# The chunked delta-rule scan: keys transposed as full tiles, with the second key operand's chunks exchanged

## The chip, the cores and the metric

One core of a Trainium2 chip runs the whole program as one launch. The metric is the device time of one execution in microseconds. Everything is float32.

## The reference, cut to what matters

The program is a model of six layers on 512 tokens (and 256 context tokens) of width 1024. The change touches one layer, an RWKV-7 mixer, whose core is a recurrence over 768 tokens, in two directions, with 16 heads of 64:

```python
def step(S, inp):
    w_t, k_t, v_t, kk_t, a_t = inp[:5]
    s_kk = jnp.einsum('nbhvk,nbhk->nbhv', S, kk_t)
    S = S * w_t[..., None, :] - s_kk[..., :, None] * (kk_t * a_t)[..., None, :] + v_t[..., :, None] * k_t[..., None, :]
    y_t = jnp.einsum('nbhvk,nbhk->nbhv', S, inp[5]) if emit else None
    return S, y_t
```

S is a 64x64 state per head. There are two kinds of keys that write into it: `k_t` (called kd below), with the value beside it, and `kk_t * a_t` (called ka below), with the difference beside it that the state is corrected by.

## The kernel before, in words

The recurrence is computed in chunks of 64 tokens. Twelve scan steps (`SCAN_STEPS`, L2286) alternate between the two directions n = 0 and n = 1; each takes a tile of 128 tokens, which is two chunks c = 0, 1 (`HALF`, L2288: columns or partitions 0 to 63 and 64 to 127). Keys lie in SBUF with features on the partitions: 8 groups p (two heads of 64 features each), and 128 tokens along the free dimension, as `KA`, `KD` (the two kinds of keys) and `AR` (kk and r), [128 x 8 x 128] each.

Per step s the work has three strands, each written as a generator on every engine, and `scan_slots` (L2343) takes their pieces in a fixed order that each engine has for itself (a string of "1", "2", "c"):

- strand 1, `chosen_*`, for step s + 2: four groups of decay sums on TensorE (L2435), exponentials on ScalarE (L2649, L2650), products of the operands with them on VectorE (L2750 kk, L2753 KA, L2759 KD, L2761 r), the matrix L from AR and KA on TensorE (L2448), its copy by ScalarE (L2659), and the inverse of its 16x16 diagonal blocks on VectorE (stream transposes L2769, small products L2780 to L2846, four scaled copies on ScalarE L2664, transposes back L2794, L2797).
- strand 2, `solved_*`, for step s + 1: the 64x64 triangular inverse from those blocks. `blocks` (masked by VectorE, L2879, and one addition on GpSimd, L2973), the series Z2 and Z3 (L2484 and 64x64 products; ScalarE copies L2676), the inverse Q (copy L2703), the Gram products `values` (L2533; masked by VectorE, L2893), and between them the two token groups, `tokens(0)` and `tokens(1)` (L2505).
- strand c, `carried_*`, for step s: the state products chunk by chunk (X, U, P, Y), with ScalarE's copies of X (L2718) and of U (L2726) and VectorE's sums into the state (L2935; scaling between steps L2925) and the output (L2943).

A token group turns the keys of one chunk c into rows of tokens, for the state product P. On TensorE it is 16 products with the identity as moving operand: the 64 columns of KD's chunk give the partitions HALF[c] of a PSUM bank, the 64 columns of KA's chunk the partitions HALF[1 - c]. Two banks (halves of the 8 groups) are filled, and ScalarE copies each with one 128x512 copy to `KB[s % 2][c]` (L2685). The value rows `VU` have the values on the partitions HALF[c] and the differences on HALF[1 - c], hence that layout. Banks of strands 1 and 2 come in turn from a ring of four (`take(pl, x, "0123")`, L250): the Z2 series of the first eight heads takes the two banks that `tokens(0)` doesn't have, that of the other eight heads takes the two of `tokens(0)` and waits (`free`) for ScalarE's copies of them. `product` is one matmul call (L334); `turned` (L338) is a transpose call (L340).

TensorE's order of the pieces is "1 1 c 2 1 1 2 c 2 c 2 2 c 1 c c 2 2 c 2 2 c 2 2 2" (L2420): decay sums, two; a state piece; `blocks(0)`; decay sums, two; `blocks(1)`; a state piece; `tokens(0)`; a state piece (U); Z2 twice; P and Y; L; X of the second chunk, twice a piece; `tokens(1)`; Z3; U; Z3; the Gram product G; P and Y; Q; the last two Gram products. ScalarE's is "1 1 1 1 c 2 c 2 2 1 c 2 2 c 2 1 2" (L2636): its token copies stand just ahead of the copies of U (L2726), those ahead of the copies of Z2.

SyncE issues the loads. `keys_sp` (L2360) waits until the last Gram product of two steps before has read the tiles, then loads ka and kd, a contiguous 4 KB on each of 128 partitions each; `rows_sp` (L2370) behind it loads kk and r in pieces of 512 B; then come a value load (L2401), the decays' load (L2357) and a value load. VectorE waits for kk at L2750 and for KA at L2753, once a step.

Of the kernel before, what the change touches and what calls it, by code (L numbers as in the profile page):

```python
# [10 lines left out]
ALU = mybir.AluOpType  # L11
ACT = mybir.ActivationFunctionType
AX = mybir.AxisListType.X

P = 128
# [245 lines left out]
def bank(pl, key):  # L261
    return pl.banks[pl.bank_of[key]]
# [59 lines left out]
def table(pl, name, lo=0, hi=None):  # L322
    at, n = pl.coff[name]
    return pl.C[:, at + lo:at + (n if hi is None else hi)]
# [7 lines left out]
def product(e, out, pairs, start=True, stop=True, loose=False):  # L332
    for i, (a, b) in enumerate(pairs):
        r = e.matmul(out, a, b, start=start and i == 0, stop=stop and i == len(pairs) - 1, skip_group_check=loose)  # L334
    return r


def turned(pl, e, out, in_):  # L338
    k = in_.shape[0]
    return e.transpose(out, in_, table(pl, "ident")[0:k, 0:k])  # L340
# [288 lines left out]
QI, KI, GL, GQ, GK, QA, KA, UC, RB, VB, VA, TILES = 0, 2, 3, 4, 5, 6, 10, 14, 16, 18, 22, 26  # L629
# [1658 lines left out]
HALF = slice(0, 64), slice(64, 128)  # L2288
# [71 lines left out]
def keys_sp(pl, e, s):  # L2360
    S_, b = pl.S, pl.scan
    n, tile = SCAN_STEPS[s]
    if s >= 2:
        e.wait_ge(*S_.gram.at(s - 2, "last"))
    for name, dst, signal in ((f"ka{n}", b.KA[s % 2], (S_.ska0, S_.ska1)[s % 2]),
                              (f"kd{n}", b.KD[s % 2], (S_.skd0, S_.skd1)[s % 2])):
        e.dma_start(dst, pl.F[name][tile].rearrange("p (m c) -> p m c", m=8)).then_inc(*signal.next(s))


def rows_sp(pl, e, s):  # L2370
# [53 lines left out]
def chosen_pe(pl, e, s, ring="0123"):  # L2424

    S_, b = pl.S, pl.scan
    n, _ = SCAN_STEPS[s]
    for j in range(4):
        at = ("decays", s, j)
        ps = take(pl, at, ring)  # L2430
        if j == 0:
            e.wait_ge(*S_.slw.at(s))
        e.wait_ge(*free(pl, at))
        for i in range(2):
            t = e.matmul(ps[:, 256 * i:256 * i + 256], b.LW[:, P * (2 * j + i):P * (2 * j + i) + P],  # L2435
                         table(pl, f"tri{n}"), start=True, stop=True)
        t.then_inc(*S_.decay_sums.next((s, j)))
        yield
    at = [("L", s, par) for par in range(2)]
    ps = [take(pl, x, ring) for x in at]  # L2440
    e.wait_ge(*S_.dve_operands.at(s, "al"))
    e.wait_ge(*S_.dve_operands.at(s, "be"))
    for par in range(2):
        e.wait_ge(*free(pl, at[par]))
    for p in range(8):
        for c in range(2):
            for par in range(2):
                t = product(e, ps[par][HALF[c], 64 * p:64 * p + 64],  # L2448
                            [(b.AR[s % 3][HALF[par], p, 0, HALF[c]], b.KA[s % 2][HALF[par], p, HALF[c]])])
    t.then_inc(*S_.gram.next((s, "L")))  # L2450
    yield


def solved_pe(pl, e, s):


    S_, b = pl.S, pl.scan
    AR, KA, KD, KB = b.AR[s % 3], b.KA[s % 2], b.KD[s % 2], b.KB[s % 2]
# [43 lines left out]
                                [(b.T16[HALF[c], 8 * g + hh, :], b.Z1[HALF[c], 8 * g + hh, :])])  # L2502
        t.then_inc(*S_.inverse_made.next((s, "Q")))

    def tokens(c):  # L2505
        names = [("tokens", s, c, hf) for hf in range(2)]
        ps = [take(pl, x, "0123") for x in names]
        if c == 0:
            e.wait_ge(*S_.dve_operands.at(s, "ka"))
        for x in names:  # L2510
            e.wait_ge(*free(pl, x))
        for p in range(8):
            o = ps[p // 4][:, P * (p % 4):P * (p % 4) + P]
            product(e, o[HALF[c], :], [(KD[:, p, HALF[c]], table(pl, "ident"))])
            t = product(e, o[HALF[1 - c], :], [(KA[:, p, HALF[c]], table(pl, "ident"))])
        t.then_inc(*S_.operands_turned.next((s, c)))

    def values(c):

        names = [("gram", s, c, par) for par in range(2)]  # L2520
        ps = [take(pl, x, "0123") for x in names]
        e.wait_ge(*S_.dve_operands.at(s, "ka" if c is None else "ro"))
        for x in names:
            e.wait_ge(*free(pl, x))
        for p in range(8):
            for i in range(2):
                for par in range(2):
                    cols = slice(64 * p, 64 * p + 64)
                    if c is None:
                        t = product(e, ps[par][HALF[i], cols], [(KD[HALF[par], p, HALF[i]],  # L2530
                                                                 AR[HALF[par], p, 0, HALF[i]])])
                    else:
                        t = product(e, ps[par][HALF[1 - c if i else c], cols],  # L2533
                                    [((KA if i else KD)[HALF[par], p, HALF[c]], AR[HALF[par], p, 1, HALF[c]])])
        t.then_inc(*S_.gram.next((s, "G") if c is None else (s, "R", c), *([(s, "last")] if c == 1 else [])))

    blocks(0)
# [131 lines left out]
def solved_act(pl, e, s):  # L2669
    S_, b = pl.S, pl.scan  # L2670

    def series(g, stage, dst):
        e.wait_ge(*S_.inverse_made.at(s, g, stage))
        for c in range(2):
            at = (stage, s, g, c)
            e.activation(dst[HALF[c], 8 * g:8 * g + 8, :], by_heads(bank(pl, at)[HALF[c], :]), ACT.Copy).then_inc(  # L2676
                *S_.act_blocks.next((s, g, stage), frees=at) if c else S_.act_blocks.next(frees=at))

    def tokens(c):
        e.wait_ge(*S_.operands_turned.at(s, c))  # L2680
        if s >= 2:
            e.wait_ge(*S_.carried.at(2 * (s - 2) + 1, "P"))
        for hf in range(2):
            at = ("tokens", s, c, hf)
            e.activation(b.KB[s % 2][c][:, 512 * hf:512 * hf + 512], bank(pl, at)[:, :], ACT.Copy).then_inc(  # L2685
                *S_.act_turned.next((s, c), frees=at) if hf else S_.act_turned.next(frees=at))

    tokens(0)
    yield
    for g in range(2):  # L2690
        series(g, "Z2", b.Z2)
        yield
    tokens(1)
    yield
    for g in range(2):
        series(g, "Z3", b.Z1)
        yield
    e.wait_ge(*S_.inverse_made.at(s, "Q"))
    if s >= 2:
        e.wait_ge(*S_.carried.at(2 * (s - 2) + 1, "U"))  # L2700
    for c in range(2):
        at = ("Q", s, c)
        e.activation(b.Q[s % 2][:, 8 * c:8 * c + 8, :], by_heads(bank(pl, at)[:, :]), ACT.Copy).then_inc(  # L2703
            *S_.act_blocks.next((s, "Q"), frees=at) if c else S_.act_blocks.next(frees=at))
    yield
# [36 lines left out]
def chosen_dve(pl, e, s):  # L2742
    S_, b = pl.S, pl.scan
    n, _ = SCAN_STEPS[s]
    AR, KA = b.AR[s % 3], b.KA[s % 2]
# [4 lines left out]
    e.tensor_tensor(AR[:, :, 0, :], AR[:, :, 0, :], b.E[:, :, 0, :], ALU.mult).then_inc(*made.next((s, "al")))  # L2750
    e.wait_ge(*S_.decayed.at(s, 3, "m"))
    e.wait_ge(*(S_.ska0, S_.ska1)[s % 2].at(s))
    e.tensor_tensor(KA, KA, b.EM, ALU.mult).then_inc(*made.next((s, "be")))  # L2753
    e.tensor_copy(b.EL[:, s % 4, :], b.E[:, :, 1, last]).then_inc(*made.next())
    e.reciprocal(b.EF[:, s % 4, :], b.E[:, :, 0, 127 - last]).then_inc(*made.next((s, "ends")))
    yield
# [1264 lines left out]
```

## Time and profile before

| | us |
|---|---|
| median of 3 runs | 4994.42 |
| lowest, highest | 4991.78, 4994.98 |
| the profiled execution | 4992.55 |
| its span, first to last instruction | 4990.7 |
| TensorE busy | 4795.9 |
| VectorE busy | 1474.0 |
| ScalarE busy | 1054.5 |

The span is what the profile's rows add up to; the execution's own time is 1.85 us longer. PE is TensorE's matmuls, PEld its weight loads (they overlap), DVE is VectorE, ACT ScalarE, POOL GpSimd, SPq the queue of SyncE that issues DMAs. A float32 product on TensorE stands as two records. In a timeline row the columns are the start, the time from the first start to the last end, engine, line, operation, tiles and shapes, count, and in brackets the idle time before it and what ended it; W and A are SBUF, C the constants, ps PSUM. The matmuls of all helpers have the helper's line, L334 or L340, so they are told apart by shapes and place.

### The profile page before, as it was taken

How to read it: one execution, taken by the hardware profiler on the slowest of the kernel's cores; microseconds unless marked ns; L12 is line 12 of the kernel's file. 1: busy time of each engine (PE TensorE's matmuls, PEld its weight loads, DVE VectorE, ACT ScalarE, POOL GpSimd, SP SyncE). 2: the span in 40 equal slices, each digit the busy share in tenths (PEclk: the TensorE clock that was granted, in tenths of full speed). 3: DMA queues.
4: the chain of work that ended last, by engine and by line, in shares of the span. 5: the costliest groups of instructions: out<-in, count | busy, mean ns of one | idle time of the engine just before them, and what ended most of it. 6: DMA issues, size and time to landing. Idle time of an engine off the chain costs nothing.

```text
span 4990.7 us, 63120 instructions
## 1 busy us (share of the span) xinstructions
PE 4795.9 (96%) x27502; PEld 2627.9 (53%) x27502; DVE 1474.0 (30%) x2777; ACT 1054.5 (21%) x2046; POOL 322.4 (6%) x302
## 2 busy tenths in 40 slices
PE   8999999999999999999999989998999999999999
PEld 4444444444444444666545568887544555544444
DVE  3621110363111010000044337775301444410100
ACT  1131000113100022111033124443211333311210
POOL 1100000020000000000003200000000011000000
PEclk9989999998999999999999999999999999999999
DMA  3151212115121211111134322222211000111211
GB/s 122 60 203 68 76 65 78 62 57 213 59 76 69 75 51 68 51 43 51 53 128 137 128 94 76 73 78 97 77 50 52 28 15 28 44 51 68 84 67 59
DMA packets 91840, 378.36 MB, mean 76 GB/s; under 512 B 7984, under 2 KB 33712, under 8 KB 62128
## 3 DMA queue, kind: packets, MB, share of 16 engines
q1 hardware_dynamic: 80608, 332.92, 18.9%
q0 software_dynamic: 9808, 37.75, 2.2%
q8 instruction: 219, 3.59, 0.3%
q10 hardware_dynamic: 1152, 3.67, 0.2%
q14 instruction: 53, 0.43, 0.0%
HBM read 334.46 MB, written 39.85 MB: 75 GB/s over the span
## 4 chain that ended last, share of the span: by engine, by line
PE 92%; DVE 4%; ACT 2%; issue 1%; DMA 0%; POOL 0%; POOLq 0%; SPq 0%; DVEq 0%; ACTq 0%
PE ps L522 43%; PE ps L334 23%; PE ps L543 7%; PE ps L3414 2%; PE ps L1782 2%; PE ps L340 1%; PE ps L3336 1%; PE ps L991 1%; PE ps L947 1%; PE ps L3425 1%; PE ps L3339 1%; PE ps L2435 1%; PE ps L2484 1%; PE ps L3335 1%; PE ps L3337 1%
## 5 line engine op out<-in xcount | busy, mean ns | idle before, releaser
L522 PE MATMUL ps<-A,W 128*128 128x512 f32 (+1 forms) x5344 | 2150.1, 562 | 23.9 <-DVE A L494 8.8
L522 PEld LDWEIGHTS ps<-A,W 128*128 128x128 f32 x5344 | 1018.0, 192 | 1105.7 <-issue 1063.4
L334 PE MATMUL ps<-A,W 64*64 64x64 f32 (+3 forms) x3264 | 660.9, 379 | 9.4 <-ACT A L3579 5.8
L334 PEld LDWEIGHTS ps<-A,W 128*128 128x128 f32 (+2 forms) x3264 | 349.0, 162 | 304.3 <-issue 280.7
L334 PEld LDWEIGHTS ps<-A 64*64 64x64 f32 (+2 forms) x8416 | 400.6, 147 | 148.7 <-issue 93.9
L334 PE MATMUL ps<-A 64*64 64x64 f32 (+3 forms) x8416 | 437.8, 237 | 41.1 <-ACT A L2650 14.1
L543 PE MATMUL ps<-W,A 128*128 128x512 f32 (+1 forms) x896 | 367.0, 571 | 1.8 <-ACT A L1568 1.8
L543 PEld LDWEIGHTS ps<-W,A 128*128 128x128 f32 x896 | 173.0, 194 | 191.2 <-issue 183.7
L436 ACT ACTIVATE A<-R 128x512 f32<-128x512 f32 (+1 forms) x96 | 52.6, 574 | 758.5 <-DVE R L1578 330.5
L1698 DVE SCALAR_TENSOR_TENSOR A<-ps,V,A 128x512 f32<-128x512 f32 (+1 forms) x48 | 31.0, 661 | 486.9 <-PE ps L334 486.3
L1578 DVE SCALAR_TENSOR_TENSOR R<-ps,MOD,R 128x512 f32<-128x512 f32 (+1 forms) x48 | 31.7, 662 | 416.5 <-PE ps L522 410.5
L3558 ACT ACTIVATE A<-ps,A 128x256 f32<-128x256 f32 (+1 forms) x128 | 84.9, 668 | 283.3 <-DVE A L3679 283.3
L1714 POOL TENSOR_TENSOR A<-A 128x1536 f32<-128x1536 f32 (+1 forms) x16 | 46.4, 2900 | 1488.9 <-ACT A L1671 1488.9
L1512 DVE TENSOR_TENSOR A<-A,ps 128x512 f32<-128x512 f32 x44 | 30.2, 688 | 334.0 <-PE ps L522 334.0
L1671 ACT ACTIVATE A<-ps 128x256 f32<-128x256 f32 (+1 forms) x96 | 50.3, 527 | 369.8 <-PE ps L522 369.7
L334 PE MATMUL ps<-W,A 64*64 64x64 f32 (+3 forms) x1472 | 117.9, 260 | 1.2 <-issue 0.8
L334 PEld LDWEIGHTS ps<-W,A 64*64 64x64 f32 (+1 forms) x1472 | 101.9, 163 | 21.7 <-issue 16.5
L3677 DVE TENSOR_REDUCE A<-ps 128x1 f32<-128x256 f32 (+1 forms) x128 | 71.4, 558 | 132.6 <-PE ps L3337 132.0
L340 PE MATMUL ps<-C,A 128*128 128x128 f32 x608 | 97.1, 284 | 10.9 <-DVE A L1250 10.3
L1479 ACT ACTIVATE A<-ps 128x512 f32<-128x512 f32 x44 | 26.3, 598 | 369.8 <-PE ps L522 369.8
L340 PEld LDWEIGHTS ps<-C,A 128*128 128x128 f32 x608 | 70.0, 141 | 60.7 <-issue 41.7
L1517 DVE TENSOR_TENSOR R<-R,ps 128x512 f32<-128x512 f32 x16 | 11.0, 688 | 300.0 <-PE ps L334 300.0
(362 smaller groups left out, 4234.8 us busy)
## 6 DMA issues: line engine op xcount, KB each, us to landing
W<-in_ada SPq DMA_DIRECT2D x48, 1024.0 KB, 5.5
W<-in_w_up SPq DMA_DIRECT2D x44, 1024.0 KB, 4.8
W<-in_w_down SPq DMA_DIRECT2D x32, 704.0 KB, 4.0
W<-in_w_in SPq DMA_DIRECT2D x18, 1024.0 KB, 4.8
W<-in_sgu_v SPq DMA_DIRECT2D x16, 1024.0 KB, 4.9
W<-in_sgu_u SPq DMA_DIRECT2D x16, 1024.0 KB, 4.8
W<-in_sgu_z SPq DMA_DIRECT2D x16, 1024.0 KB, 4.8
W<-in_sgu_o SPq DMA_DIRECT2D x16, 1024.0 KB, 4.8
```

The lines of the kernel that those rows point to most:

```text
L334: r = e.matmul(out, a, b, start=start and i == 0, stop=stop and i == len(pairs) - 1, skip_group_check=loose)
L340: return e.transpose(out, in_, table(pl, "ident")[0:k, 0:k])
L436: e.activation(pl.sq[k % 2][:, cols], pl.R[:, k, cols], ACT.Square).then_inc(*S_.act_squares.next((key, k, seg[0])))
L522: t = e.matmul(ps, w[:, k, c:c + mc], x(k, seg), start=k == 0, stop=k == kt - 1)
L543: mm = e.matmul(ps, x(k0 + k, tile), w[:, k, :], start=k0 + k == 0, stop=k0 + k == kt - 1)
L947: e.matmul(ps, b.qa[o:o + 64, pair, P * i:P * i + P], b.ka[o:o + 64, pair, 0:L], start=True, stop=True).then_inc(*S_.att_scores.next((l, n)))
L991: t = e.matmul(ps[32 * k:32 * k + 32, :], b.cs[:, 4 * hf + k, :], w[:, k, :], start=hf == 0, stop=hf == 1)
L1671: e.activation(dst[:, m, o:o + seg[1]], bank(pl, at)[:, 0:seg[1]], func).then_inc(*signal.next((i, g), frees=at) if m == 1 and seg is segs ...
L1782: t = e.matmul(y, w[:, k, :], b.x(k, s), start=k == 0, stop=k == 7)
L3414: t = e.matmul(ps[:, :], uq[j][:, k, 0:P], b.cq[:, k, :], start=k == 0, stop=k == 5)
L3558: e.activation(b.pr[:, z, lo:hi], bank(pl, at)[:, 0:hi - lo], ACT.Exp, bias=m[:, 2:3], scale=b.rq[:, p % 2, 2 * i + j:2 * i + j + 1], accu ...
L3677: e.tensor_reduce(m[:, part:part + 1], bank(pl, at)[:, 0:w], AX, ALU.max).then_inc(*made.next())
```

## The change

A token group no longer stands for a chunk but for half of the key groups (hf): four groups p, each turned by two full 128x128 transposes (`turned`), KD into one bank and KA into another. For KA's rows to come out on the partitions HALF[1 - c], KA is loaded with its two chunks exchanged: two DMAs instead of one, each of pieces of 64 tokens (256 B). What reads KA follows: the product with the exponentials is cut into two halves, and L and the Gram products read the exchanged half. ScalarE copies each bank in two halves of 64 partitions, as the halves go to different `KB[..][c]`: four copies a group instead of two.

```diff
@@ -2362,9 +2362,11 @@
     n, tile = SCAN_STEPS[s]
     if s >= 2:
         e.wait_ge(*S_.gram.at(s - 2, "last"))
-    for name, dst, signal in ((f"ka{n}", b.KA[s % 2], (S_.ska0, S_.ska1)[s % 2]),
-                              (f"kd{n}", b.KD[s % 2], (S_.skd0, S_.skd1)[s % 2])):
-        e.dma_start(dst, pl.F[name][tile].rearrange("p (m c) -> p m c", m=8)).then_inc(*signal.next(s))
+    ka, signal = pl.F[f"ka{n}"][tile].rearrange("p (m c) -> p m c", m=8), (S_.ska0, S_.ska1)[s % 2]
+    for c in range(2):
+        e.dma_start(b.KA[s % 2][:, :, HALF[1 - c]], ka[:, :, HALF[c]]).then_inc(*signal.next(s) if c else signal.next())
+    e.dma_start(b.KD[s % 2], pl.F[f"kd{n}"][tile].rearrange("p (m c) -> p m c", m=8)).then_inc(
+        *(S_.skd0, S_.skd1)[s % 2].next(s))
 
 
 def rows_sp(pl, e, s):
@@ -2446,7 +2448,7 @@
         for c in range(2):
             for par in range(2):
                 t = product(e, ps[par][HALF[c], 64 * p:64 * p + 64],
-                            [(b.AR[s % 3][HALF[par], p, 0, HALF[c]], b.KA[s % 2][HALF[par], p, HALF[c]])])
+                            [(b.AR[s % 3][HALF[par], p, 0, HALF[c]], b.KA[s % 2][HALF[par], p, HALF[1 - c]])])
     t.then_inc(*S_.gram.next((s, "L")))
     yield
 
@@ -2502,18 +2504,18 @@
                                 [(b.T16[HALF[c], 8 * g + hh, :], b.Z1[HALF[c], 8 * g + hh, :])])
         t.then_inc(*S_.inverse_made.next((s, "Q")))
 
-    def tokens(c):
-        names = [("tokens", s, c, hf) for hf in range(2)]
+    def tokens(hf):
+
+        names = [("tokens", s, hf, k) for k in range(2)]
         ps = [take(pl, x, "0123") for x in names]
-        if c == 0:
+        if hf == 0:
             e.wait_ge(*S_.dve_operands.at(s, "ka"))
         for x in names:
             e.wait_ge(*free(pl, x))
-        for p in range(8):
-            o = ps[p // 4][:, P * (p % 4):P * (p % 4) + P]
-            product(e, o[HALF[c], :], [(KD[:, p, HALF[c]], table(pl, "ident"))])
-            t = product(e, o[HALF[1 - c], :], [(KA[:, p, HALF[c]], table(pl, "ident"))])
-        t.then_inc(*S_.operands_turned.next((s, c)))
+        for p in range(4):
+            for k, keys in enumerate((KD, KA)):
+                t = turned(pl, e, ps[k][:, P * p:P * p + P], keys[:, 4 * hf + p, :])
+        t.then_inc(*S_.operands_turned.next((s, hf)))
 
     def values(c):
 
@@ -2530,8 +2532,9 @@
                         t = product(e, ps[par][HALF[i], cols], [(KD[HALF[par], p, HALF[i]],
                                                                  AR[HALF[par], p, 0, HALF[i]])])
                     else:
-                        t = product(e, ps[par][HALF[1 - c if i else c], cols],
-                                    [((KA if i else KD)[HALF[par], p, HALF[c]], AR[HALF[par], p, 1, HALF[c]])])
+                        to = HALF[1 - c if i else c]
+                        t = product(e, ps[par][to, cols],
+                                    [((KA if i else KD)[HALF[par], p, to], AR[HALF[par], p, 1, HALF[c]])])
         t.then_inc(*S_.gram.next((s, "G") if c is None else (s, "R", c), *([(s, "last")] if c == 1 else [])))
 
     blocks(0)
@@ -2676,14 +2679,16 @@
             e.activation(dst[HALF[c], 8 * g:8 * g + 8, :], by_heads(bank(pl, at)[HALF[c], :]), ACT.Copy).then_inc(
                 *S_.act_blocks.next((s, g, stage), frees=at) if c else S_.act_blocks.next(frees=at))
 
-    def tokens(c):
-        e.wait_ge(*S_.operands_turned.at(s, c))
+    def tokens(hf):
+        e.wait_ge(*S_.operands_turned.at(s, hf))
         if s >= 2:
             e.wait_ge(*S_.carried.at(2 * (s - 2) + 1, "P"))
-        for hf in range(2):
-            at = ("tokens", s, c, hf)
-            e.activation(b.KB[s % 2][c][:, 512 * hf:512 * hf + 512], bank(pl, at)[:, :], ACT.Copy).then_inc(
-                *S_.act_turned.next((s, c), frees=at) if hf else S_.act_turned.next(frees=at))
+        for k in range(2):
+            at = ("tokens", s, hf, k)
+            for c in range(2):
+                to = HALF[1 - c if k else c]
+                e.activation(b.KB[s % 2][c][to, 512 * hf:512 * hf + 512], bank(pl, at)[to, :], ACT.Copy).then_inc(
+                    *S_.act_turned.next(*([(s, hf)] if k else []), frees=at) if c else S_.act_turned.next())
 
     tokens(0)
     yield
@@ -2750,7 +2755,9 @@
     e.tensor_tensor(AR[:, :, 0, :], AR[:, :, 0, :], b.E[:, :, 0, :], ALU.mult).then_inc(*made.next((s, "al")))
     e.wait_ge(*S_.decayed.at(s, 3, "m"))
     e.wait_ge(*(S_.ska0, S_.ska1)[s % 2].at(s))
-    e.tensor_tensor(KA, KA, b.EM, ALU.mult).then_inc(*made.next((s, "be")))
+    for c in range(2):
+        x = KA[:, :, HALF[1 - c]]
+        e.tensor_tensor(x, x, b.EM[:, :, HALF[c]], ALU.mult).then_inc(*made.next((s, "be")) if c else made.next())
     e.tensor_copy(b.EL[:, s % 4, :], b.E[:, :, 1, last]).then_inc(*made.next())
     e.reciprocal(b.EF[:, s % 4, :], b.E[:, :, 0, 127 - last]).then_inc(*made.next((s, "ends")))
     yield
```

## Rows read from the trace of the kernel before

**Rows 1.** The page: busy time of each engine; the ending chain by engine.

```profile
PE 4795.9 (96%) x27502; PEld 2627.9 (53%) x27502; DVE 1474.0 (30%) x2777; ACT 1054.5 (21%) x2046; POOL 322.4 (6%) x302
...
PE 92%; DVE 4%; ACT 2%; issue 1%; DMA 0%; POOL 0%; POOLq 0%; SPq 0%; DVEq 0%; ACTq 0%
```

**Rows 2.** One window: PE, PEld, DVE, ACT, POOL busy, clock, DMA share, GB/s.

```profile
3080.00:3120.00 40.00, 37.26 (x965) 33.01 (x966) 32.47 (x55) 17.72 (x36) 2.18 (x2) 1.00 0.24 67
```

**Rows 3.** Chain that ended last, two scan steps: start, duration, what.

```profile
3097.60 0.03 ACT A L2659
...
3124.71 0.14 issue
...
3151.30 1.72 ACT A L2664 x4
```

**Rows 4.** Timeline around the first token group, and one group of copies.

```profile
3087.78 1.97 PE L334 MATMUL ps<-C,W 128*64 128x128 f32 x32
...
3089.68 0.97 PE L334 MATMUL ps<-A 64*64 64x64 f32 x26
3089.79 1.09 ACT L2685 ACTIVATE A<-ps 128x512 f32<-128x512 f32 x2 [3.17 <-PE ps L334]
...
3090.90 1.08 ACT L2726 ACTIVATE A<-ps 64x512 f32<-64x512 f32 x2
...
3092.29 0.60 PE L2484 MATMUL ps<-C 64*64 64x512 f32 x1
...
3092.66 1.21 ACT L2676 ACTIVATE A<-ps 64x512 f32<-64x512 f32 x2 [0.68 <-PE ps L334]
...
L2676 ACT ACTIVATE A<-ps 64x512 f32<-64x512 f32 x96 | 56.8, 592 | 33.2 <-PE ps L334 32.0
```

**Rows 5.** Timeline: second token group, and the ends of two steps.

```profile
3101.35 1.97 PE L334 MATMUL ps<-C,W 128*64 128x128 f32 x32
...
3115.90 1.97 PE L2435 MATMUL ps<-C,A 128*128 128x256 f32 x8 [1.20 <-DVE A L2893]
...
3150.48 0.69 DVE L2846 TENSOR_REDUCE A<-A 128x64 f32<-128x512 f32 x1
...
3157.53 1.97 PE L2435 MATMUL ps<-C,A 128*128 128x256 f32 x8 [0.93 <-DVE A L2893]
```

**Rows 6.** Timeline of the features stage: full transposes between matmuls.

```profile
2797.47 0.82 PE L340 MATMUL ps<-C,A 128*128 128x128 f32 x6
2798.13 2.31 PE L334 MATMUL ps<-A,W 128*128 128x512 f32 x5
```

**Rows 7.** Timeline of VectorE: products of other sizes, and its wait.

```profile
3106.11 1.03 DVE L2834 TENSOR_TENSOR A<-A 128x512 f32<-128x512 f32 x1
...
3134.76 1.41 DVE L2925 TENSOR_TENSOR A<-A 64x512 f32<-64x512 f32 x2
3137.60 1.40 DVE L2935 TENSOR_TENSOR A<-A,ps 64x512 f32<-64x512 f32 x2 [1.44 <-PE ps L334]
```

**Rows 8.** Loads: KB, us to landing; their issue and their first user.

```profile
A<-f_kk SPq DMA_DIRECT2D x4, 512.0 KB, 8.0
...
W<-f_kk SPq DMA_DIRECT2D x1, 512.0 KB, 6.1
W<-f_r SPq DMA_DIRECT2D x1, 512.0 KB, 7.9
...
3116.04 0.56 SPq L2377 DMA_DIRECT2D W<-f_kk  x1
...
3129.86 1.23 DVE L2750 TENSOR_TENSOR W<-W,A 128x1024 f32<-128x1024 f32 x1
```

**Rows 9.** TensorE's first block products in two steps; one window.

```profile
3118.92 2.10 PE L334 MATMUL ps<-A 64*64 64x64 f32 x64
...
3411.79 3.56 PE L334 MATMUL ps<-A 64*64 64x64 f32 x64 [1.76 <-DVE A L2893]
...
3410.00:3420.00 10.00, 5.21 (x104) 5.04 (x105) 6.36 (x10) 0.00 (x0) 1.08 (x1) 0.78 0.01 2
```

## The prediction, made before the changed kernel was built

> **What bounds the kernel now.** I read the page first: TensorE is busy for 96% of the span and holds 92% of the chain that ended last [rows 1]. An average over stages says nothing of one stage, so next come windows over the scan. It runs from about 2870 to 3470 us, in twelve steps of some 42 us; in an ordinary stretch of 40 us TensorE is busy 37, at full granted clock, VectorE 32 and ScalarE 18 [rows 2]. The third view is the chain of waits through two steps, with the timeline of single engines beside it [rows 3 to 5]. In each step it has two parts. From the decay sums (3115.90) to the solve's input matrix L, the chain stays on TensorE, and the first token group (`tokens(0)`) lies in it. From ScalarE's copy of L (3097.60) to the next decay sums it lies on VectorE and ScalarE: the blocks' inverse, four scaled copies (L2664), the transposes, and a masking (L2893) that frees a PSUM bank for the decay sums. The second token group (`tokens(1)`, from 3101.35) lies under that part in the steps of direction 1. In the steps of direction 0 VectorE's inverse is shorter, and the chain comes to L2664 by way of TensorE and ScalarE's series copies, but only just: VectorE had its result at 3150.48 + 0.69 = 3151.17 and ScalarE began L2664 at 3151.30 [rows 3, 5]. So time saved in `tokens(0)` should reach the end, and time saved in `tokens(1)` mostly turns into idle TensorE ahead of the decay sums.
>
> **Turning the keys.** A token group is 16 products of 128x64 keys with the identity; a float32 product stands as two records, so 32 records. They start at 3087.78 and the next group at 3089.68: 1.90 us, 59 ns a record. The second group (3101.35) takes the same 1.97 us to its last end [rows 4, 5]. The new group is 8 calls of `turned` on full 128x128 tiles. Six such calls exist in the features stage: six records, 0.82 us to the last end, and the next matmul starts 0.66 us after the first, so 0.110 us each [rows 6]. There a call is one record, each with other data. Eight take 0.88 us: 1.02 us less a group. The bounds: zero gain if the tile cost what 8 x 2 records of 128x256 pace do (1.97/8 = 0.246 us for 256 columns [rows 5], half of it for 128, so 16 x 0.123 = 1.97 us), and 1.02. I take 1.02, since [rows 6] show this very form.
>
> **Copies on ScalarE.** Two copies 128x512 a group (a pair in 1.09 us) become four of 64x512. Pairs of this size take 1.08 us where both write the same half of the partitions (L2726) and 1.21 where they alternate (L2676) [rows 4]. One alone is 0.59 us, so one follows another every 0.49 to 0.62 us. In the first group the transposes would end at 3087.78 + 7 x 0.11 + 0.27 = 3088.82, ScalarE starts at 3088.86, and four copies end between 3090.92 (3 x 0.49 + 0.59) and 3091.31 (3 x 0.62 + 0.59). Before, they ended at 3090.88. Queued behind them on ScalarE are the U copies (L2726), so these start at most 0.4 us later than 3090.90, and the state products that want them start well after 3092.29. The second Z2 series takes the two banks that the copies free. TensorE reaches it at 3092.29 now, at 3091.27 then; a bank comes free 0.14 us after the copy (the step from ScalarE to TensorE in the chain, [rows 3]), at 3091.06 to 3091.45. The new wait is 0 to 0.18 us; I take 0.09. After `tokens(1)` the same sum gives a wait only in time that is idle anyway. The copy of L (3097.60) follows TensorE. So **tokens(0)** gives 12 x (1.02 - 0.09) = 11.2 us.
>
> **tokens(1)** gives 0.1 us in each of some five steps of direction 0 (3151.30 less 3151.17, [rows 5]), nothing in those of direction 1, and its whole 1.0 in the last solved step, which has no step behind it whose inverse VectorE would work on: 1.5 us.
>
> **VectorE.** The product KA*EM, 1.22 us, is cut in two of 128x512. Above, two products over half the partitions take 1.40 us (L2925), so 0.2 us more; the farthest row, a 128x512 product of another pattern (L2834), takes 1.03, two of them 0.84 us more. Behind it stand the Q and state scalings, and then VectorE waits 1.44 us for TensorE (3137.60, [rows 7]); with that wait shorter by 0.93 there is 0.5 left, so 0.2 costs nothing and 0.84 would cost 0.34 a step, 4 us in all. I take 0.2, as the pieces of 256 bytes lie side by side in the same tiles. The Gram products change only which half of KA they read: same shapes, same count.
>
> **Loads.** One issue more on SP a step, and its 128 packets of 4 KB become 2 x 1024 of 256 B. Behind them on SP's queue stand kd, kk, r and the values. Of those, kk (1024 packets of 512 B, issued at 3116.04) landed after 6.1 us, and r, issued 0.6 us behind it, after 7.9 [rows 8]; so such a load adds 2.4 us to the queue. Two halves at that price, less nothing for the load they replace, are 4.8 us late; at the price of bytes nearly none. kk landed at 3122.1 and is wanted at 3129.86 (L2750), so 7.7 us of cover, and 5.8 by the median landing of 8.0 [rows 8]; ka, issued first, and r, wanted later, have more. Cost 0; a microsecond of lateness beyond the cover would cost a microsecond a step. The values are issued a step ahead, and the decays' load waits for TensorE to 3123.82.
>
> **Clock.** The idle time of TensorE before the decay sums is 1.20 us in one direction, 0.93 in the other [rows 5]; it grows to some 2.2 and 1.8. No ordinary step shows a lower clock now. But in the last solved step TensorE was idle for 1.76 us before 3411.79, the granted clock went to its lower level (1.2 GHz; 0.78 mean over 3410 to 3420) and 64 records took 3.56 us where they take 2.10 otherwise: 1.46 us lost, on the chain [rows 9]. So some steps will now pay: between none and all twelve. The one fall had 1.76 us of idle time before it, and none came after 1.20; I take three steps, at 1.1 us each since part falls on idle time: 3.3 us.
>
> By the Trainium skill (TensorE: Matmul & The Clock Gate, Part 4, PE-mode transpose) transposes on TensorE do not count as activity for the clock gate as matmuls do. No row here shows it: the transposes of [rows 6] stand between dense matmuls. It speaks against this change: by it the sum would go towards rival C, by the rows it stands.
>
> **The sum.** 11.2 + 1.5 - 3.3 = 9.4 us. The profiled execution took 4992.55 us (span 4990.7), so 4983.2; the median of the runs shown is 1.9 above it, so 4985.1. I predict 4985.
>
> **Rivals.** (A) *The clock stays up*: TensorE's longer idle time is spread over two places and the level never falls. Gain 12.7, 4981.7. For it: the 37 of 40 us busy. Against it: the fall behind 1.76 us of idle time. 0.27. (B) *ScalarE becomes the bound*, or VectorE's cut product does: the second Z2 series waits for banks, and the copy of L moves by half or less. At 0.6 us or more lost a step the gain is 0 to 5; 4989 to 4994. Against it: ScalarE has 0.68 us of idle time before the next L2676 pair [rows 4]. 0.14; a transpose dearer than in [rows 6] is in here too. (C) *The clock pays at every step*: with half the records in the token groups the lower level comes in each step, once or twice. At 12 to 20 times 1.46 the 12.7 are turned into a loss of 5 to 16: 5000 to 5010; with eight times, a gain of 1: 4993. 0.09. The page named above is what this rival rests on if transposes count for nothing. (D) *The slower side by the loads*: kk comes after VectorE is ready at L2750. It decides from 5.8 us of added queue time on. At twice the 2.4 us for each half, 9.6 less 1.3 for the replaced packets is 8.3, late by 2.5 a step, 30 a run, against 9.4 gained: 5005. For it: packets of 256 B exist nowhere in these loads. Against it: nothing shows twice the price. 0.05. The Trainium skill (DMA: Bandwidth & Descriptors, the table at its head) says that below 512 B the engines read, modify and write.
>
> **How the numbers follow.** Forecast 0.45 (own range 4981 to 4988), A 0.27, B 0.14, C 0.09, D 0.05. A measurement of this kernel tells some 0.2%, 10 us, from no change. Faster by more: all of A and a good third of the forecast's, 0.43. Slower by more: D and about half of C, 0.09. The rest, 0.48, is within. The range 4979 to 4995 takes in A with 2 us beside it, the forecast, B and the mild end of C.
>
> **What would show it.** 576 TensorE records fewer (24 x 24); `turned` groups of 8 in 0.88 us at L340; ScalarE four copies in 2.1 to 2.5 us; step period down from 42 to about 41.2; idle before the decay sums near 2 us; granted clock under 1 in a few steps; kk landing one to five us later, with VectorE at L2750 still released by ScalarE. Wrong if the period is unchanged, if L2750 waits for a DMA, or if the clock in the scan falls everywhere.

## The result, and the profile after

The changed kernel takes 4986.05 us (median of 20 runs, 4976.62 to 4992.24); the kernel before, in 20 runs beside it, 4992.58. The ratio is 0.9986, interval 0.9979 to 0.9992: 6.5 us faster (4 to 10 by the interval), less than the 10 us that I called telling. The profiled execution took 4983.66 us, its span is 4981.9.

The page of the changed kernel, busy times and chain by engine (answers to [rows 1]):

```profile
PE 4775.0 (96%) x26926; PEld 2606.3 (52%) x26926; DVE 1474.1 (30%) x2789; ACT 1080.2 (22%) x2094; POOL 322.4 (6%) x302
...
PE 90%; DVE 6%; ACT 2%; issue 2%; DMA 0%; POOL 0%; POOLq 0%; DVEq 0%; ACTq 0%; SPq 0%
```

TensorE has 576 records fewer, ScalarE 48 more, as the change says. The chain has moved from TensorE to VectorE by 2% of the span.

The timeline around the first token group, the same step as [rows 4]:

```profile
3082.01 1.04 PE L340 MATMUL ps<-C,W 128*128 128x128 f32 x8
...
3082.99 0.97 PE L334 MATMUL ps<-A 64*64 64x64 f32 x26
3083.09 2.31 ACT L2690 ACTIVATE A<-ps 64x512 f32<-64x512 f32 x4 [2.14 <-PE ps L340]
3083.28 1.29 DVE L2760 TENSOR_TENSOR A<-A 128x512 f32<-128x512 f32 x2
...
3085.42 1.08 ACT L2731 ACTIVATE A<-ps 64x512 f32<-64x512 f32 x2
...
3085.60 0.60 PE L2486 MATMUL ps<-C 64*64 64x512 f32 x1
...
3088.87 1.40 DVE L2942 TENSOR_TENSOR A<-A,ps 64x512 f32<-64x512 f32 x2 [0.36 <-PE ps L334]
```

The next group starts 0.98 us after the first transpose; before, it started 1.90 us after the first product. ScalarE's four copies take 2.31 us. The second Z2 series starts 3.59 us after the token group began, 4.51 before (3092.29 - 3087.78): 0.92 us saved. VectorE's cut product takes 1.29 us instead of 1.22 (L2753 before), and VectorE still waits 0.36 us for TensorE afterwards, where it waited 1.44 us in the same step before.

How far does that carry? A yardstick inside the scan is the time from the first to the last copy of L by ScalarE, twelve pairs of copies; the instructions of that line, with their first and last start, in the kernel before and the changed one:

```profile
L2659 ACT ACTIVATE A<-ps x24: 591/594/603, 2902.3 to 3392.6; 128x512 f32<-128x512 f32 x24
```

```profile
L2662 ACT ACTIVATE A<-ps x24: 588/594/605, 2897.3 to 3380.6; 128x512 f32<-128x512 f32 x24
```

490.3 and 483.3 us: 7.0 us less. Over the whole scan, from its first decay sums to the first product of the output stage, it is 578.8 us against 586.2, 7.4 less. The profiled pair differs by 8.8 us in span: 5.0 stand ahead of the scan already, in code that is the same, 7.4 are the scan, and 3.6 are given back behind it, in the same code again. Such drift is in every execution, and most of it goes with the granted clock: over the 20 runs of the changed kernel the four at a mean clock of 0.977 took 4990.2 us on average, the three at 0.980 took 4977.8. So the experiments below are read by three things: the ratio, the yardstick, and the profile's own events.

An undisturbed pair of steps takes 40.49 + 41.04 = 81.5 us now and took 83.7 (41.64 + 42.07). Ten steps at that rate would have gained 11 us between the second and the last copy of L; 6.8 arrived (419.8 to 413.0 us). Two kinds of events took 5.4 us in the changed kernel. (The kernel before had 1.3 us of the first kind too; that comes below.) The first, TensorE's timeline in a step that is late by 1.9 us:

```profile
3028.87 1.81 PE L334 MATMUL ps<-A 64*64 64x64 f32 x52
...
3032.20 0.62 PE L334 MATMUL ps<-A 64*64 64x64 f32 x12 [1.52 <-issue]
```

In the middle of the first block products, after 52 of 64 records, TensorE does nothing for 1.52 us, and the profile shows no semaphore or bank that it waits for. (A smaller gap of this kind, 0.70 us, stands ahead of the decay sums of 3109; that step is 0.4 us late.) The second kind is seen in TensorE's decay sums later on, eight records that take 1.97 us otherwise:

```profile
3191.14 2.77 PE L2437 MATMUL ps<-C,A 128*128 128x256 f32 x8 [1.01 <-DVE A L2900]
```

Two windows there and in the next step (time in the window, busy times by engine with their instructions, then granted clock, DMA share, GB/s):

```profile
3192.00:3196.00 4.00, 4.00 (x56) 3.15 (x55) 2.76 (x5) 1.74 (x4) 0.00 (x0) 0.57 1.12 293
3233.00:3237.00 4.00, 4.00 (x22) 2.82 (x24) 3.59 (x6) 1.20 (x3) 0.00 (x0) 0.57 1.05 263
```

The granted clock is 0.57 on average over these windows: for most of them it is at the lower of the two levels (1.2 GHz of 2.4). Just before the first fall TensorE had stood idle for 0.49, 0.74 and 1.01 us. The idle time alone doesn't foretell a fall: ahead of the decay sums of 3109 there were 0.49, 0.70 and 1.01 us, and the clock stayed up. The two steps are 1.4 and 1.7 us late. In the profile of the kernel before, none of the ordinary steps (those between 3000 and 3400 us) showed a fall.

The loads, to landing, in the step of 3109:

```profile
W<-f_kk SPq DMA_DIRECT2D x1, 512.0 KB, 6.8
W<-f_r SPq DMA_DIRECT2D x1, 512.0 KB, 8.9
```

0.7 and 1.0 us later than in [rows 8]. No instruction of VectorE waits for them.

### The profile page after: what moved, and what is told of

Same layout as the page of the kernel before. It is cut to its first block, busy times and chain, and to the rows that moved or that the text cites. A ratio compares the mean times of both kernels' runs of the same rounds, so it can differ in the third digit from the quotient of the medians.

```text
span 4981.9 us, 62040 instructions
## 1 busy us (share of the span) xinstructions
PE 4775.0 (96%) x26926; PEld 2606.3 (52%) x26926; DVE 1474.1 (30%) x2789; ACT 1080.2 (22%) x2094; POOL 322.4 (6%) x302
## 4 chain that ended last, share of the span: by engine, by line
PE 90%; DVE 6%; ACT 2%; issue 2%; DMA 0%; POOL 0%; POOLq 0%; DVEq 0%; ACTq 0%; SPq 0%
PE ps L522 43%; PE ps L334 21%; PE ps L543 7%; PE ps L3421 2%; PE ps L1782 2%; PE ps L340 2%; PE ps L3343 1%; PE ps L991 1%; PE ps L947 1%; PE ps L3432 1%; PE ps L2437 1%; PE ps L3346 1%; PE ps L3342 1%; PE ps L3344 1%; PE ps L450 0%
## 5 line engine op out<-in xcount | busy, mean ns | idle before, releaser
L340 PE MATMUL ps<-C,A 128*128 128x128 f32 x704 | 109.6, 282 | 12.9 <-DVE A L1250 10.3
L340 PEld LDWEIGHTS ps<-C,A 128*128 128x128 f32 x704 | 80.8, 142 | 63.0 <-issue 43.3
```

## The experiments

Each was run beside the kernel before on one chip; the ratio is to that. All times of a yardstick are of one profiled execution. They are in three rounds: what the change costs and where TensorE's gap is from; which group pays; what the clock does.

### The loads alone

The kernel before, with this in `keys_sp`:

```diff
     ...
+    for c in range(2):
+        e.dma_start(b.KA[s % 2][:, :, HALF[c]], ka[:, :, HALF[c]]).then_inc(*signal.next(s) if c else signal.next())
```

> The kernel before, with ka loaded by two DMAs of 256-byte pieces (chunks not exchanged); nothing else changed. My theory: the longer burst of small packets now and then holds TensorE up in the middle of a group, without any wait of its own (idle time put down to issue, as the 1.52 us in the changed kernel's profile at 3032.20), some 0 to 2 us at a few steps, so 1 to 4 us slower than before and the scan (586.2 us from its first decay sums to the first product of the output stage in the profile of before) 587 to 590 us. Rival: the loads cost nothing and such gaps are chance, scan 585.5 to 586.5 us. Second rival, of the prediction: kk comes late at the first product of VectorE; then that product would wait for a DMA.

Ratio 1.0006 (0.9992 to 1.002). The scan is 585.8 us (586.2 before), inside the rival's range. Nine of ten steps take what they take before, to 0.3 us; one is late by 1.6 us, by a fall of the clock at 3366.7, behind a wait for VectorE and not behind a load. **My theory of the burst fell**: the profile shows no cost of the pieces. (The ratio alone would leave room for some microseconds.) The halves land 4.0 us after their issue, nothing waits for them, and the rival of the late kk is out too.

### The copies alone

The kernel before with four copies a group:

```diff
         for hf in range(2):
             at = ("tokens", s, c, hf)
-            e.activation(b.KB[s % 2][c][:, 512 * hf:512 * hf + 512], bank(pl, at)[:, :], ACT.Copy).then_inc(
+            for i in range(2):
+                to = HALF[1 - i if hf else i]
+                e.activation(b.KB[s % 2][c][to, 512 * hf:512 * hf + 512], bank(pl, at)[to, :], ACT.Copy).then_inc(
                     ...
```

> The kernel before, with each of ScalarE's token copies of 128x512 cut in two of 64x512 (four a group). My theory: the group of copies takes 2.31 us instead of 1.09, the copies of U behind it start 1.2 us later, and the second Z2 series finds its banks free at 3089.79 + 2.31 + 0.14 = 3092.24 against 3092.29, so it hardly waits: 0 to 0.1 us a step, at most 1 us in all. Rival: ScalarE is the bound once it has these copies (the copies of Z2 and L come later), 0.5 us a step or more, 6 us or more in all.

Ratio 0.9994 (0.9984 to 1.0005). Steps take 41.6 and 42.0 us as before, but for one with a fall of the clock (3201.1) and one that is 1.1 us late, the same step that is 0.9 us late in the kernel before. The copies show no cost.

### All of the change but the transposes

```diff
-                t = turned(pl, e, ps[k][:, P * p:P * p + P], keys[:, 4 * hf + p, :])
+                for i in range(2):
+                    t = product(e, ps[k][HALF[i], P * p:P * p + P], [(keys[:, 4 * hf + p, HALF[i]], table(pl, "ident"))])
```

> The changed kernel, but each full transpose made by two products with the identity as before (32 records a group); loads, copies and VectorE's cut product as in the change. My theory: this is the change's cost without its gain: 2 to 5 us slower than before (0 to 1 from the copies, the rest from the loads), scan 587 to 591 us. Rival, that the change's gain was only small because clock falls follow from TensorE's longer idle time: without the transposes the idle time is as before, so this kernel would be within 1 us of before.

This is the changed kernel with each full transpose made by two products. Ratio 0.9991 (0.9979 to 1.0002), yardstick 492.7 us with one fall of the clock. My 2 to 5 us were wrong; the interval takes in the rival's forecast. Loads, copies and the cut product together show no cost, and what is lost of the gain comes with the transposes.

### The exchange made by the stores

The changed kernel with a contiguous load of KA in the scan, and in the features stage:

```diff
             ...
+            for c in range(2):
+                e.dma_start(dst[:, :, HALF[1 - c]], src[:, :, HALF[c]]).then_inc(*out.next(m) if c else out.next())
```

> The changed kernel, but the chunks of ka are exchanged when the features stage stores it (two DMAs of 256-byte pieces on the GpSimd queue), and the scan loads it with one contiguous DMA. My theory: TensorE's gaps without a wait in the key burst are gone, the scan is 575 to 577 us (578.8 with the change), and the features stage is unchanged if GpSimd's issues are hidden: 2 to 4 us faster than the change, 8.5 to 11 faster than before. Rival (loads cost nothing): the same as the change, scan 578 to 579 us. If the features stage's GpSimd queue is not hidden, that stage grows by up to 1 us for each of 16 stores.

Ratio 0.9992 (0.9981 to 1.0002), yardstick 484.2 us: no better than the change. My theory was wrong here too; the gaps are still there. TensorE's timeline in the step where the change had its gap:

```profile
3033.19 1.81 PE L334 MATMUL ps<-A 64*64 64x64 f32 x52
...
3036.52 0.62 PE L334 MATMUL ps<-A 64*64 64x64 f32 x12 [1.52 <-issue]
```

The loads are other ones, and the gap is the same to 0.01 us, after the same 52 records. What the two kernels share is TensorE's program. That points to the place in the program, and the last experiment of the next round moved it. A second such gap shows in this run: 1.75 us in the block products, ending at 3120.27. The decay sums behind it ran at the lower clock (3.63 us), and the step was 3.7 us late. So a gap of the first kind can be followed by a fall of the clock as a wait can.

### The first group alone, the second alone

The line of the third experiment, with the full transposes kept for `hf == 0` or for `hf == 1`.

> The changed kernel, but only the first token group is turned by full transposes, the second by the products as before. My theory (the first group lies on the chain, the second beside VectorE's inverse): it keeps nearly the whole gain of an undisturbed step, 0.9 us for a step of direction 0 or 1 (41.64 and 42.07 us from one copy of L to the next become about 40.8 and 41.2), 83.7 to about 82.0 a pair, where the full change has 81.7. Rival (both groups count alike): half of the gain, 82.7 a pair.

> The changed kernel, but only the second token group is turned by full transposes. My theory: 0.1 us in each step of direction 0, nothing in those of direction 1, so 83.6 us a pair (83.7 before), with TensorE's idle time before the decay sums 1 us longer. Rival: half of the gain, 82.7 a pair.

The first group alone: ratio 0.9981 (0.9972 to 0.9989), yardstick 480.3 us. Its undisturbed steps take 40.63 and 41.05 us, 81.7 a pair: 2.0 of the 2.2 us that the whole change gains a pair. The missing 0.14 us is in the steps of direction 0 (40.49 in the change). No ordinary step has a fall of the clock and no gap stands in the block products, but three gaps ahead of decay sums (1.32, 1.32 and 1.01 us) make steps late by 0.9, 0.4 and 0.5 us. The ratio doesn't tell this kernel from the whole change (0.9979 to 0.9992).

The second group alone: ratio 1.0019 (1.001 to 1.0028), **slower than before by 0.2%**, yardstick 501.9 us against 490.3. Neither theory had that. Its undisturbed steps of direction 0 take 41.50 us, 0.14 less than before, so the group does save what was forecast for it; all five steps of direction 1 and one of direction 0 are late by a fall of the clock. The decay sums of one of its steps, and a window across them (busy times, then granted clock):

```profile
3198.15 3.65 PE L2437 MATMUL ps<-C,A 128*128 128x256 f32 x8 [1.25 <-DVE A L2904]
...
3198.00:3202.00 4.00, 3.85 (x16) 2.74 (x18) 3.76 (x7) 1.03 (x3) 0.00 (x0) 0.57 0.98 231
```

3.65 us for what takes 1.97. The profile's clock is at its lower level in this way six times between 3020 and 3380 us, each time at the decay sums or the block products behind them, where the chain is.

The last solved step can show the price too. Its block products, where [rows 9] had 3.56 us at the lower clock: the first two lines are of the changed kernel, the others of the one with the first group alone:

```profile
3399.71 3.21 PE L334 MATMUL ps<-A 64*64 64x64 f32 x64 [2.42 <-DVE A L2900]
3405.95 3.71 PE L334 MATMUL ps<-A 64*64 64x64 f32 x64 [3.03 <-DVE A L2886]
...
3399.71 2.10 PE L334 MATMUL ps<-A 64*64 64x64 f32 x64 [1.41 <-DVE A L2904]
3404.85 2.10 PE L334 MATMUL ps<-A 64*64 64x64 f32 x64 [3.03 <-DVE A L2890]
```

From the last copy of L to the output stage the changed kernel takes 77.0 us, the kernel before 77.3 and this one 73.3. How much of that is the kernel's and how much this execution's is open: the first group alone with the copies in the other order (the last experiment) had a fall of the clock there and took 75.2.

### The copies in another order

```diff
+        for i, (k, c) in enumerate(((0, 0), (1, 1), (0, 1), (1, 0))):
             ...
```

> The changed kernel with ScalarE's four copies of a group in the order that takes the same half of the partitions twice running. My theory (the banks' release holds the second Z2 series up by 0.15 us a step): the four copies take 2.2 us instead of 2.31, their end is 0.1 us earlier, and a pair takes 81.5 us instead of 81.7, 1 us in all. Rival (the wait for the banks is no bound): the same pair.

Ratio 0.9988 (0.998 to 0.9997). The four copies take 2.18 us instead of 2.31, and the second Z2 series starts 3.59 us after the token group, as in the change. The banks were not the bound: the rival's case. (The yardstick, 480.2 us, is better than the change's because this execution had no fall of the clock in ordinary steps; the gap after 52 records is there again, with 1.24 us of idle time.)

### TensorE's program moved by 128 instructions

```diff
-        for p in range(8):
+        for p in chain(range(8) if s == 0 and c == 1 else (), range(8)):
```

> The changed kernel with 128 more instructions on TensorE in the first solved step, in time in which it is idle (the last Gram products made twice, the first pass overwritten). TensorE's gaps without a wait stand at one place in each 256 of its instructions, and its program comes in packets of 16 KB by a queue of the same DMA engines. My theory: the gap of 1.52 us in the first block products of one step (3032.20) is such a fetch, late in the burst of key loads, on the chain by where the 256 fall; moved by half of 256, the steps of 7.74 us from the first to the third decay sum are gone and those that fall elsewhere are on idle time: scan 1.5 to 2.5 us shorter unless the clock falls more often. Rival (the gap belongs to the loads or to chance): the gap is in the same products again, or in none of a pattern of 256.

Ratio 0.9977 (0.9969 to 0.9986), 4981.16 us, the lowest of the ratios, though its interval overlaps the change's (0.9979 to 0.9992). TensorE in the step of the gap:

```profile
3029.66 1.97 PE L2437 MATMUL ps<-C,A 128*128 128x256 f32 x8 [2.01 <-DVE A L2900]
...
3032.68 2.10 PE L334 MATMUL ps<-A 64*64 64x64 f32 x64
```

The 64 records run through in 2.10 us. From the first to the third decay sum that step takes 5.89 us where the change had 7.74; yardstick 480.2 us, with a fall of the clock in one step. So the gap goes when the program is moved, and 128 more instructions, made in idle time, didn't make the kernel slower. In this step they save 1.9 us; the profiled scan is 5 us shorter (573.8 us against 578.8), the rest by one fall of the clock less and events behind the last copy of L. Whether the median time is shorter the ratios don't tell.

What waits there is shown by one more view. The DMA queue of the instructions in 3 us around the gap of the changed kernel:

```profile
q1 hardware_dynamic: 1426, 0.97, 100.9%
q8 instruction: 1, 0.02, 2.2%
```

One packet of 16 KB stands among 1426 packets of loads. In the whole run of the kernel before this queue brings 219 packets while 56231 instructions of TensorE run (27502 matmuls, as many weight loads, 1227 of its sequencer), 257 a packet; in the changed kernel it is 215 for 55079, 256 a packet. Counted in this way, all 102 gaps of over 0.25 us without a wait in the scans of the thirteen kernels, between 2970 and 3400 us, stand at one place in each 256 instructions, to one instruction, and each ends 1.2 to 1.6 us after a packet of this queue has ended. So what TensorE waits for is its own next instructions. Each kernel has five to twelve of them. The kernel before has six, in the last products ahead of the decay sums, where TensorE would otherwise wait, and three reach the chain. This is the one that costs most, in the step that is 0.9 us late:

```profile
3241.09 0.79 PE L334 MATMUL ps<-A 64*64 64x64 f32 x34 [1.23 <-issue]
3241.81 1.99 PE L2435 MATMUL ps<-C,A 128*128 128x256 f32 x8
```

The decay sums follow with no wait: the gap has used up the idle time that stands here in other steps, and more. The packet before the change's gap started at 3029.7 and took 1.05 us, and TensorE went on 1.5 us later. Why it started no sooner (the one before it began at 3021.1) is argued, not shown: the burst of key loads of 3025 to 3034 may be the reason, contiguous or in pieces.

### The idle time filled

The last Gram products of a step get 16 products ahead of them that they overwrite, so nothing of the result changes:

```diff
-        for p in range(8):
+        for p in chain(range(4) if c == 1 else (), range(8)):
```

> The kernel with only the second group by full transposes (which came out slower than before, with the granted clock at its lower level in six ordinary steps), plus 16 Gram products more a step (32 records, 1.05 us), made just before the last ones and overwritten, in the time in which TensorE waits for the decay sums' bank. My theory: the second group's transposes only trade work for idle time, and the idle time brings the clock down; filled again, the falls in ordinary steps go from six to none to two, a pair of steps takes 83.6 to 84.2 us, and the kernel is 6 to 9 us faster than without the filling, level with before. Rival (transposes do not count for the clock, however long the idle time): the falls stay, four or more.

Ratio 0.9999 (0.999 to 1.0008) where the same kernel without the filling had 1.0019. Windows over the ordinary steps, first of the kernel with only the second group turned, then of the same with the filling:

```profile
3000.00:3100.00 100.00, 91.30 (x2261) 79.83 (x2258) 76.53 (x130) 47.74 (x96) 4.36 (x4) 0.98 0.25 69
3100.00:3200.00 100.00, 89.28 (x2363) 78.30 (x2360) 80.24 (x143) 47.34 (x95) 4.36 (x4) 0.97 0.26 70
3200.00:3300.00 100.00, 89.87 (x2159) 78.43 (x2159) 74.74 (x126) 43.77 (x90) 6.54 (x6) 0.97 0.34 91
3300.00:3400.00 100.00, 90.85 (x2237) 79.20 (x2233) 74.85 (x129) 46.38 (x93) 4.36 (x4) 0.95 0.24 63
```

```profile
3000.00:3100.00 100.00, 91.62 (x2359) 80.54 (x2356) 77.01 (x138) 49.19 (x99) 4.35 (x4) 1.00 0.27 69
3100.00:3200.00 100.00, 89.97 (x2477) 79.77 (x2472) 80.59 (x134) 45.74 (x94) 4.90 (x5) 1.00 0.31 85
3200.00:3300.00 100.00, 91.91 (x2368) 80.77 (x2368) 78.18 (x133) 47.34 (x96) 5.99 (x6) 1.00 0.28 76
3300.00:3400.00 100.00, 92.23 (x2489) 81.45 (x2480) 80.44 (x143) 49.61 (x100) 4.36 (x4) 1.00 0.26 66
```

The clock column goes from 0.95 to 0.98 to 1.00 throughout. A pair takes 83.6 us, though one step is 1.5 us late by a gap of 1.84 us; the yardstick is 490.9. It is not one execution's chance: over the eleven runs of each kernel the mean clock is 0.978 without the filling and 0.981 with it, where the kernel before has 0.980 in both rounds. The transposes are the same in both, so they don't bring the clock down where the idle time around them is filled. Idle time and a lack of counted work aren't told apart by this, as the filling mends both. The filling also moves TensorE's program, but the decay sums at 1.96 us instead of 3.65 are the clock's.

> The changed kernel with the same 16 overwritten Gram products a step. My theory: fewer falls of the clock than the change's two in ordinary steps; and as they move TensorE's stream by 64 instructions a step, the long first block products (7.74 us) move too or go. Scan 572 to 577 us (578.8 with the change), 2 to 6 us faster than the change. Rival (the clock is no part of the loss): as the change, or slower by what the 1.05 us cannot hide.

The changed kernel filled: ratio 0.9985 (0.9977 to 0.9994), yardstick 478.2 us, the shortest of all, every ordinary step at 40.5 or 41.1 us, no fall and no long block products. The gaps for instructions are still there, but lie in idle time. In the profile that is 5 us better than the change; the ratio does not tell the two apart.

### The first group alone, with the copies in the other order

> Only the first group by full transposes (the best so far: scan 572.2 us), and ScalarE's copies in the order that takes the same half of the partitions twice running. My theory: 0.02 to 0.1 us a step more where the second Z2 series waits for the banks; scan 571.5 to 572.5 us, 10 to 12 us faster than before. Rival (copies still bind): nothing gained, or a bank's later release costs it again.

Ratio 0.9984 (0.9975 to 0.9993), yardstick 481.2 us: nothing gained, as the order of the copies binds nothing. One step had the long block products again (after 48 records, 1.70 us of idle time at 3197.8), at another multiple of 256 instructions.

## Why the prediction was right or wrong, point by point

The time (4985 against 4986.05) and the class (within 0.2%) came out as forecast, though not all by the terms of the sum. That the time is met to 1.1 us is partly luck: the gain is 6.5 us where I had 9.4, and the kernel before takes 4992.58 in 20 runs where I had started from 4994.42, the median of three. One number of the working is wrong: 30 us of lateness in rival D give 5015, not 5005, and no row shows its 1.3 us for the replaced packets; the rival did not come true.

**tokens(0)**, 11.2 us: right in size, wrong in one of its two parts. I had 1.02 us less the 0.09 of a wait for banks. The saving measured is 0.92 to the next group already: transposes start every 0.11 us as in [rows 6], but the last of the eight takes 0.20 us until the products in 64x64 tiles start, so the group takes 0.98 us and not 0.88. The wait for banks isn't there, which the reordered copies showed. Two errors of 0.1 us cancelled: luck. That the first group lies on the chain, the first-group kernel showed.

**tokens(1)**, 1.5 us: right in the ordinary steps, where it saves 0.14 us in direction 0 (I had 0.1) and nothing in direction 1. The 1.0 us in the last solved step isn't to be seen. From the start of its `tokens(0)` to the output stage the kernel before takes 44.5 us (3469.45 less 3424.91) and the changed one 44.2 (3457.08 less 3412.91): 0.4 saved, where both groups should have brought 1.9. Behind the last Gram products TensorE now waits 1.45 us for VectorE (L2950) at 3441.72, which it didn't before. And its price was not zero. I wrote that time saved there "mostly turns into idle TensorE", and put the idle time's cost under the clock for the change as a whole; the runs show that it belongs to this group: alone it makes the kernel 0.2% slower.

**Clock**, 3.3 us in three steps: two falls in ordinary steps, 1.4 and 1.7 us, 3.1 in all, so the term held. That more idle time brings the falls fits the filled kernels. The kernel before isn't free of it: three kernels with its idle time (pieces, copies, all but transposes) each had one fall in ordinary steps. So what the change adds is a little less than I charged. Rival C, with a fall at every step, came true only for the second group alone, six in ten steps. The Trainium skill says in TensorE: Matmul & The Clock Gate (Part 4, PE-mode transpose) that transposes don't count as activity as matmuls do. The runs neither need it nor refute it: with the same transposes and 32 records of products in the idle time the falls went from six to none, which either cause allows. Whether transposes count for less than products was not measured.

**The term that was missing** is the instruction fetch: 1.9 + 0.4 us in two ordinary steps, on the chain because of where the change moved the 256-instruction marks. No step of the prediction looked at it, though the kernel before pays for it too: its steps of 3014, 3223 and 3266 are 0.2, 0.9 and 0.4 us late behind such gaps ahead of the decay sums. So the change adds some 0.8 us of it, not 2.3. With it the account of the ten steps closes. Before: five pairs of 83.7, and 1.3 us of events (0.2, 0.9, 0.4, less 0.2 by which the first of the ten steps is shorter than the others), 419.8 us. Changed: five pairs of 81.5 and 5.4 us of events (1.9, 0.4, 1.4, 1.7), 413.0. The filled kernel, in which neither kind reaches the chain, takes 407.8.

**VectorE and ScalarE** were right: 0.07 us for the cut product (0.2 taken), hidden; the copies 2.31 us (2.06 to 2.45). **Loads** were right: no cost is seen. The Trainium skill has in DMA: Bandwidth & Descriptors (Specifications) that below 512 B the engines read, modify and write, on which rival D rested. Here packets of 256 B took 18 ns and packets of 512 B 27 ns (medians over the loads of the step of 3109), more for a byte but not twice as much. kk lands 0.7 us later, and the kernel with the pieces alone has ratio 1.0006, so for this load it does not matter.

**What would show it**: the record count and the kk landing were as written; the step period too, 40.5 and 41.0 instead of 41.2 on average. The idle time before the decay sums is near 2 us, but not in one piece: it is 1.01 us at 3109.22, with two other pieces of 0.49 and 0.70 ahead of it.

## What to carry to other kernels

Work taken off TensorE while another engine holds the chain isn't free: it becomes idle time of TensorE. Where that idle time stands just ahead of the point at which the chain comes back to TensorE, the clock can fall, and then work on the chain takes nearly twice as long (3.65 us for 1.97). So look first at changing only the part on the chain. It gave as much as the whole change here (0.9981 against 0.9986; the intervals overlap, so it isn't shown to be faster). If idle time must grow, cheap products in it can keep the clock up (1.0019 went to 0.9999 for the second group). And where TensorE runs many small products, look at gaps put down to issue in the middle of a group: their place follows the instruction count, so a change that only shortens the program can move one onto the chain.

## What the runs showed of the hardware that was not expected

- A gap without a wait stands after the same 52 records of a group in kernels with other loads (1.52 us in both), and is gone when 128 instructions are added 50 us earlier. In thirteen kernels, 102 such gaps stand at one place in each 256 TensorE instructions and end 1.2 to 1.6 us after a 16 KB packet of the instruction queue.
- Full float32 transposes start every 0.11 us, whatever follows; the last takes 0.20 us until a product in 64x64 tiles starts (0.98 us for eight) and 0.11 until one in full tiles does.
- Two ScalarE copies of 64x512 out of PSUM follow each other every 0.50 us where they write the same 64 partitions and every 0.60 to 0.62 where they change halves: four take 2.31 us with two changes, 2.18 with one.
- With the second group alone, the lower clock came back in six of ten steps, and with 1.05 us of products in the idle time in none. A fall came after 0.49, 0.74 and 1.01 us of idle time, and none after 0.49, 0.70 and 1.01 in an earlier step of the same execution.
